# Half of the gate/up pairs of two SwiGLU up projections by seven block products in place of eight

## The reference, cut to what matters

```python
def rms_norm_2(x, g):
    xf = x.astype(jnp.float32)
    y = xf * lax.rsqrt(jnp.mean(xf * xf, axis=-1, keepdims=True) + RMS_EPS)
    return (y * g.astype(jnp.float32)).astype(x.dtype)

def swiglu_ffn(h, w13, w2):
    g, u = jnp.split(h @ w13, 2, axis=-1)
    return (jax.nn.silu(g) * u) @ w2

h = h + swiglu_ffn(rms_norm_2(h, conv_ffn_norm_g[i]), conv_ffn_w13[i], conv_ffn_w2[i])
h = h + swiglu_ffn(rms_norm_2(h, mla_ffn_norm_g[j]), mla_ffn_w13[j], mla_ffn_w2[j])
```

## Time and profile before

| | |
|---|---|
| Time, median of three runs | 1853.58 us (1853.45 to 1859.59) |
| The profiled execution's own time | 1854.15 us |
| Its span, first to last instruction | 1852.3 us |
| TensorE busy | 1821.4 us, 98% |
| VectorE, ScalarE, GpSimd busy | 50%, 39%, 11% |
| Granted TensorE clock, mean | 0.997 of full |
| DMA, mean | 87 GB/s |
| Up stage of feed-forward two | about 923 to 1163 us |
| Up stage of feed-forward three | about 1480 to 1721 us |

### The profile page before, as it was taken

How to read it: one execution, slowest core, us unless ns; L and a number is a source line. 1 busy time by engine, 2 the same in 40 slices (tenths; PEclk the granted TensorE clock), 3 DMA queues, 4 the chain that set the end, 5 groups by cost and what they waited for, 6 DMA issues and landing times.

```text
span 1852.3 us, 27361 instructions
## 1 busy us (share of the span) xinstructions
PE 1821.4 (98%) x10063; PEld 1474.8 (80%) x10063; DVE 918.4 (50%) x1280; ACT 716.5 (39%) x1059; POOL 203.5 (11%) x178
## 2 busy tenths in 40 slices
...
DMA packets 309228, 161.03 MB, mean 87 GB/s; under 512 B 12688, under 2 KB 306832, under 8 KB 309024
## 3 DMA queue, kind: packets, MB, share of 16 engines
...
## 4 chain that ended last, share of the span: by engine, by line
PE 96%; DVE 2%; ACT 1%; issue 1%; DMA 0%; ACTq 0%; DVEq 0%
PE ps L372 28%; PE ps L374 28%; PE ps L373 28%; PE ps L1796 1%; PE ps L1207 1%; PE ps L2109 1%; PE ps L2110 1%; PE ps L1787 1%; PE ps L1118 1%; PE ps L1524 1%; PE ps L940 1%; PE ps L1468 1%; PE ps L1512 0%; PE ps L1893 0%; PE ps L1894 0%
## 5 line engine op out<-in xcount | busy, mean ns | idle before, releaser
L372 PE MATMUL ps<-xhi,whi 128*128 128x512 f32 x1656 | 653.6, 395 | 2.3 <-ACT mx L1442 1.2
L374 PE MATMUL ps<-xhi,wlo 128*128 128x512 f32 x1656 | 645.3, 390 | 0.0
L373 PE MATMUL ps<-xlo,whi 128*128 128x512 f32 x1656 | 645.0, 389 | 0.0
L359 ACT ACTIVATE whi<-raw 128x1024 fp32r<-128x1024 f32 (+2 forms) x297 | 309.0, 1040 | 709.3 <-PE ps L374 708.8
L367 DVE TENSOR_TENSOR wlo<-raw,whi 128x1024 fp32r<-128x1024 f32 (+2 forms) x297 | 365.5, 1231 | 270.0 <-ACT whi L359 270.0
L372 PEld LDWEIGHTS ps<-xhi,whi 128*128 128x128 f32 x1656 | 311.0, 188 | 70.8 <-issue 4.4
L373 PEld LDWEIGHTS ps<-xlo,whi 128*128 128x128 f32 x1656 | 311.1, 188 | 65.9 <-issue 3.4
L374 PEld LDWEIGHTS ps<-xhi,wlo 128*128 128x128 f32 x1656 | 311.0, 188 | 65.2
L638 DVE TENSOR_TENSOR zS<-ps,rs 128x512 f32<-128x512 f32 x132 | 91.3, 692 | 293.1 <-PE ps L374 284.3
L374 PE MATMUL ps<-h_hi,wlo 128*128 128x512 f32 x528 | 205.4, 389 | 0.0
L372 PE MATMUL ps<-h_hi,whi 128*128 128x512 f32 x528 | 205.4, 389 | 0.0
...
## 6 DMA issues: line engine op xcount, KB each, us to landing
raw<-in_conv_ffn_w SPq DMA_DIRECT2D x52, 512.0 KB, 3.8
raw<-in_mla_ffn_w SPq DMA_DIRECT2D x52, 512.0 KB, 3.9
raw<-in_w_up SPq DMA_DIRECT2D x44, 512.0 KB, 3.8
raw<-in_w_in SPq DMA_DIRECT2D x28, 512.0 KB, 3.8
raw<-in_conv_w_in SPq DMA_DIRECT2D x24, 512.0 KB, 3.8
...
```

What stands on the lines that cost most here:

```text
L359: a.activation(whi[:, u % PARTS, 0:n], raw[:, u % RAW, 0:n], ACT.Copy).then_inc(hi_split, 1)
L372: t_.matmul(out, wh, xh, start=first, stop=False)
L373: t_.matmul(out, wh, xl, start=False, stop=False)
L374: return t_.matmul(out, wl, xh, start=False, stop=last)
```

## The change

Both up stages now take their pairs alternately in two ways. Of 22 pairs, the first two and the last two are multiplied as before, and between them a loop of nine passes (`SEVEN_END` = 10) takes one plain pair and one by `pe_seven`. There, the gate and the up unit form a 2x2 block matrix with the halves of the model dimension (`g0`, `g1`, `u0`, `u1`: four slices, 512 elements each), the activations another with the two halves of the tokens (256 each), and Strassen's method in Winograd's form needs seven products m1 to m7 of blocks in place of eight. Each is 4 slices x 3 matmuls on 256 columns.

- Weight sums, per pass: VectorE makes four sums of half units and the remainders, ScalarE two roundings (`dve_w_sums`, `dve_gate_lo`, `dve_last_sum_lo`, `act_seven`).
- x sums t1 to t4, once per stage, from `xT` and the gain, each 4 slices x 256 columns (`act_x_sums`, `dve_x_sums`), then rounding and remainder (`act_x_sums_hi`, `dve_x_sum_lo`). ScalarE does the sums and the rounding of t1, t3, t2 ahead of `act_rstd`, that of t4 inside the stage.
- Block sums, per pass: ScalarE copies m1 out of PSUM, VectorE adds seven times 256 columns, then scales twice by `rs` (`dve_seven`). The seven results lie in the six ring banks of PSUM.
- The products go in fp32 to `h`. The x sums (in the last eight tiles of `h`), `t_hi`, `t_lo`, `w_hi` and `w_lo` lie where `h` and its rounded part come to lie, so rounding (`act_product_hi`, ScalarE) and remainder (`pool_products_late`, POOL, in place over `h`) of all 22 products come behind the loop, during the last four units. The down stages read them there.
- Feed-forward three uses the same buffers as two; its own (`h3_hi`, `h3_lo`) are gone.

The functions below are new; the calls in the engines' lists change accordingly. The calls of feed-forward three change in the same way as those of two, which stand at the end.

```diff
+def w_part(buf, more, u, name):
+    g0, u0 = buf[:, u % PARTS, :], buf[:, (u + 1) % PARTS, :]
+    return {"g0": g0[:, 0:HU], "g1": g0[:, HU:UNIT], "s3": u0[:, 0:HU], "u1": u0[:, HU:UNIT],
+            "s1": more[:, 0, :], "s2": more[:, 1, :], "s4": more[:, 2, :]}[name]
+def x_part(name):
+    if name in X_SUMS:
+        n = X_SUMS.index(name)
+        return [b[:, n, :, :] for b in (t_hi, t_lo)]
+    k0, c0 = {"x11": (0, 0), "x21": (4, 0), "x22": (4, HT)}[name]
+    return [b[:, k0:k0 + 4, c0:c0 + HT] for b in (xhi, xlo)]
+def seven_bank(stage, n):
+    b, at = {"m1": (0, 0), "m6": (1, 0), "m2": (1, HT), "m5": (2, 0), "m3": (3, 0), "m7": (4, 0), "m4": (5, 0)}[n]
+    return ring(S.bank(f"{stage} bank{b}"))[:, at:at + HT]
+def pe_seven(pe, stage, it):
+    u, n0 = FIRST[stage] + 2, TILE0[stage]
+    def multiply(n, w, x):
+        (xh, xl), wh, wl = x_part(x), w_part(whi, w_hi, u, w), w_part(wlo, w_lo, u, w)
+        for k in range(4):
+            cols = slice(k * P, (k + 1) * P)
+            last = passes(seven_bank(stage, n), wh[:, cols], wl[:, cols], xh[:, k, :], xl[:, k, :],
+                          k == 0, k == 3)
+        return last
+    pe.wait_ge(acc_free, n0 + 2 + 4 * it)
+    pe.wait_ge(sums_lo, nth(stage, it, 2) + 2)
+    multiply("m1", "g0", "x11").then_inc(block_done, 1)
+    multiply("m6", "s2", "t2")
+    multiply("m5", "s1", "t1").then_inc(block_done, 1)
+    multiply("m2", "g1", "x21").then_inc(unit_used, 1)
+    pe.wait_ge(lo_split, u + 4 * it + 1)
+    multiply("m3", "s4", "x22").then_inc(block_done, 1)
+    pe.wait_ge(lo_split, u + 4 * it + 2)
+    multiply("m7", "s3", "t3").then_inc(block_done, 1)
+    multiply("m4", "u1", "t4").then_inc(unit_used, 1)
+def pe_up_seven(pe, stage, name, gain, residual):
+    n0 = TILE0[stage]
+    pe_pair(pe, stage, 0, None, False, parts_of(gain), lambda: pe_sum(pe, name, NORM0[residual]))
+    for n in range(NRING):
+        pe_ring(pe, f"{stage} bank{n}")
+        S.at[f"{stage} bank{n} taken"] = ("acc_free", n0 + 2 * FT + 2)
+    pe_pair(pe, stage, 2, None, True)
+    for n in X_SUMS:
+        pe.wait_ge(*after(f"{stage} {n} lo"))
+    with pe.Fori(1, SEVEN_END) as it:
+        pe_pair(pe, stage, 0, it, False)
+        pe_seven(pe, stage, it)
+    for odd in range(2):
+        pe_pair(pe, stage, 4 * SEVEN_END + 2 * odd, None, odd)
+def act_x_sums(act, stage, gain):
+    act.wait_ge(unit_used, FIRST[stage])
+    act.wait_ge(acc_free, TILE0[stage] + 2)
+    for k in range(4):
+        last = a.activation(tf["t3"][:, k, :], xT[:, k, HT:T], ACT.Copy, scale=par(gain, k))
+    last.then_inc(*step("act", f"{stage} x12"))
+    act.wait_ge(*after(f"{stage} d1"))
+    for k in range(4):
+        last = a.activation(tf["t1"][:, k, :], tf["t1"][:, k, :], ACT.Copy, scale=par(gain, k))
+    last.then_inc(*step("act", f"{stage} t1"))
+def act_x_sums_hi(act, stage, names):
+    for n in names:
+        act.wait_ge(*after(f"{stage} {n}"))
+        a.activation(t_hi[:, X_SUMS.index(n), :, :], tf[n], ACT.Copy).then_inc(*step("act", f"{stage} {n} hi"))
+def dve_x_sums(dve, stage, gain):
+    dve.wait_ge(unit_used, FIRST[stage])
+    dve.wait_ge(acc_free, TILE0[stage] + 2)
+    v.tensor_tensor(tf["t1"], xT[:, 0:4, HT:T], xT[:, 0:4, 0:HT],
+                    ALU.subtract).then_inc(*step("dve", f"{stage} d1"))
+    for name, c0, less, ready in (("t3", HT, "t3", "x12"), ("t2", HT, "t1", "t1"), ("t4", 0, "t2", "t2")):
+        dve.wait_ge(*after(f"{stage} {ready}"))
+        for k in range(4):
+            last = v.scalar_tensor_tensor(tf[name][:, k, :], xT[:, 4 + k, c0:c0 + HT], par(gain, 4 + k),
+                                          tf[less][:, k, :], ALU.mult, ALU.subtract)
+        last.then_inc(*step("dve", f"{stage} {name}"))
+def dve_x_sum_lo(dve, stage, n):
+    dve.wait_ge(*after(f"{stage} {n} hi"))
+    at = X_SUMS.index(n)
+    v.tensor_tensor(t_lo[:, at, :, :], tf[n], f32(t_hi[:, at, :, :]),
+                    ALU.subtract).then_inc(*step("dve", f"{stage} {n} lo"))
+def act_seven(act, stage, it, zS, yg):
+    u, n0 = FIRST[stage] + 2, TILE0[stage]
+    split_hi(act, u - 1, it, 4)
+    act.wait_ge(sums_made, nth(stage, it, 4) + 2)
+    a.activation(w_hi[:, 0:2, :], xg[:, :, :], ACT.Copy).then_inc(sums_hi, 1)
+    split_hi(act, u, it, 4)
+    act_silu_gate(act, stage, 0, it, 0, zS, yg)
+    act.wait_ge(sums_made, nth(stage, it, 4) + 4)
+    a.activation(w_hi[:, 2, :], raw[:, u % RAW, HU:UNIT], ACT.Copy).then_inc(sums_hi, 1)
+    split_hi(act, u + 1, it, 4)
+    act.wait_ge(block_done, nth(stage, it, 4) + 1)
+    a.activation(kept["m1"], seven_bank(stage, "m1"), ACT.Copy).then_inc(block_kept, 1)
+    split_hi(act, u + 2, it, 4)
+    act_silu_gate(act, stage, 2, it, 1, zS, yg)
+def act_up_seven(act, stage, h, h_hi, zS, yg):
+    u0 = FIRST[stage]
+    a.preload_act_table_set("silu_and_others")
+    for j in range(4):
+        if j < 3:
+            split_hi(act, u0 + j + 2)
+        if j % 2 == 0:
+            act_silu_gate(act, stage, j, None, j // 2, zS, yg)
+        if j == 0:
+            act_x_sums_hi(act, stage, ("t4",))
+    with act.Fori(1, SEVEN_END) as it:
+        act_seven(act, stage, it, zS, yg)
+    u = 4 * SEVEN_END
+    split_hi(act, u0 + u + 1)
+    for j, tiles in enumerate((range(0, 6), range(6, 12), range(12, 17), range(17, 21))):
+        for m in tiles:
+            act_product_hi(act, stage, m, h, h_hi)
+        split_hi(act, u0 + u + j + 2)
+        if j % 2 == 0:
+            act_silu_gate(act, stage, u + j, None, j // 2, zS, yg)
+    act_product_hi(act, stage, FT - 1, h, h_hi)
+def pool_products_late(pool, stage, h, h_hi, h_lo):
+    for m in range(FT):
+        pool.wait_ge(prod_hi, PAIR0[stage] + m + 1)
+        g.tensor_tensor(h_lo[:, m, :], h[:, m, :], f32(h_hi[:, m, :]), ALU.subtract).then_inc(prod_lo, 1)
+def dve_w_sums(dve, stage, it):
+    u = FIRST[stage] + 2
+    gate, up = raw[:, u % RAW, :], raw[:, (u + 1) % RAW, :]
+    for n in range(2):
+        dve.wait_ge(unit_loaded[(u + n) % RAW], in_loop(LOADED[u + n], it, 64 // RAW))
+    v.tensor_tensor(xg[:, 0, :], up[:, 0:HU], up[:, HU:UNIT], ALU.add).then_inc(sums_made, 1)
+    dve.wait_ge(sums_made, nth(stage, it, 4) + 1)
+    v.tensor_tensor(xg[:, 1, :], xg[:, 0, :], gate[:, 0:HU], ALU.subtract).then_inc(sums_made, 1)
+    v.tensor_tensor(up[:, 0:HU], gate[:, 0:HU], up[:, 0:HU], ALU.subtract).then_inc(sums_made, 1)
+    dve.wait_ge(sums_hi, nth(stage, it, 2) + 1)
+    v.tensor_tensor(w_lo[:, 0:2, :], xg[:, :, :], f32(w_hi[:, 0:2, :]), ALU.subtract).then_inc(sums_lo, 1)
+def dve_gate_lo(dve, stage, it):
+    u = FIRST[stage] + 2
+    part = raw[:, u % RAW, HU:UNIT]
+    dve.wait_ge(hi_split, u + 4 * it + 1)
+    v.tensor_tensor(wlo[:, u % PARTS, :], raw[:, u % RAW, :], f32(whi[:, u % PARTS, :]),
+                    ALU.subtract).then_inc(sums_lo, 1)
+    dve.wait_ge(sums_lo, nth(stage, it, 2) + 2)
+    v.tensor_tensor(part, part, xg[:, 1, :], ALU.subtract).then_inc(sums_made, 1)
+def dve_last_sum_lo(dve, stage, it):
+    u = FIRST[stage] + 2
+    dve.wait_ge(sums_hi, nth(stage, it, 2) + 2)
+    v.tensor_tensor(w_lo[:, 2, :], raw[:, u % RAW, HU:UNIT], f32(w_hi[:, 2, :]),
+                    ALU.subtract).then_inc(lo_split, 1)
+def dve_seven(dve, stage, it, h, zS, yg):
+    u = FIRST[stage] + 2
+    d0, a0 = nth(stage, it, 4), nth(stage, it, 7)
+    split_lo(dve, u - 1, it, 4)
+    dve_w_sums(dve, stage, it)
+    dve_up_unit(dve, stage, 0, it, 0, 0, zS)
+    dve_gate_lo(dve, stage, it)
+    dve_last_sum_lo(dve, stage, it)
+    dve_up_unit(dve, stage, 0, it, 1, 0, zS)
+    dve_product(dve, stage, 0, it, 0, h, zS, yg)
+    split_lo(dve, u + 1, it, 4)
+    dve.wait_ge(block_kept, nth(stage, it, 1) + 1)
+    dve.wait_ge(unit_used, u + 4 * it + 1)
+    v.tensor_tensor(kept["u2"], seven_bank(stage, "m6"), kept["m1"], ALU.add).then_inc(block_added, 1)
+    v.tensor_tensor(zS[:, 0, 0:HT], seven_bank(stage, "m2"), kept["m1"], ALU.add).then_inc(block_added, 1)
+    dve.wait_ge(block_added, a0 + 1)
+    v.tensor_tensor(kept["u4"], seven_bank(stage, "m5"), kept["u2"], ALU.add).then_inc(block_added, 1)
+    split_lo(dve, u + 2, it, 4)
+    dve.wait_ge(block_done, d0 + 3)
+    dve.wait_ge(block_added, a0 + 3)
+    v.tensor_tensor(zS[:, 0, HT:T], seven_bank(stage, "m3"), kept["u4"], ALU.add).then_inc(block_added, 1)
+    dve.wait_ge(block_added, a0 + 4)
+    v.tensor_tensor(zS[:, 0, :], zS[:, 0, :], rs[:, :], ALU.mult).then_inc(acc_free, 1)
+    dve.wait_ge(block_done, d0 + 4)
+    v.tensor_tensor(kept["u3"], seven_bank(stage, "m7"), kept["u2"], ALU.add).then_inc(block_added, 1)
+    dve.wait_ge(block_added, a0 + 5)
+    v.tensor_tensor(zS[:, 1, HT:T], seven_bank(stage, "m5"), kept["u3"], ALU.add).then_inc(block_added, 1)
+    dve.wait_ge(unit_used, u + 4 * it + 2)
+    v.tensor_tensor(zS[:, 1, 0:HT], seven_bank(stage, "m4"), kept["u3"], ALU.add).then_inc(block_added, 1)
+    dve.wait_ge(block_added, a0 + 7)
+    v.tensor_tensor(zS[:, 1, :], zS[:, 1, :], rs[:, :], ALU.mult).then_inc(acc_free, 1)
```

(57 more changed lines are left out.)

49 lines of the change are left out of this document (39 added, 10 removed).

## The result

| | before | changed |
|---|---|---|
| Median (lowest to highest), runs | 1854.09 us (1853.45 to 1859.59), 6 | 1864.81 us (1860.70 to 1870.79), 6 |
| Profiled execution, its span | 1854.15, 1852.3 us | 1870.79, 1868.7 us |
| Busy TensorE, VectorE, ScalarE, GpSimd | | 98, 58, 41, 12% |
| Granted clock, mean | 0.997 | 0.99 |

What follows compares the result with a forecast made beforehand. TensorE's matmul time, or a new wait of TensorE, was taken to bound the kernel. 1854.15 − 14.4 (pairs) + 14.95 (stands) + 3.4 (low clock) = 1858.1 us, range 1843 to 1870.

Steps and rivals of the forecast that it cites:

- slower by over 0.5%: Whole kernel: outcome given chance 0.28, from POOL, weight loads, VectorE, and longer starts or low clock.
- within 0.5%: Whole kernel: outcome given chance 0.57, a time that measurement cannot tell from no change (9.3 us).
- a stand at a down stage's first tile: Down stages: TensorE waiting at the first output tile, named beforehand as a sign that the prediction is wrong.
- Spacing c: Loop: time between starts of 256-column matmuls, taken as 0.120 us, making a pass 20.96 us.
- Gain of 18 pairs: Loops of both up stages: a pair takes 10.08 us instead of 10.88, saving 14.4 us over 18.
- First stands: Ahead of unit 2 in each up stage: TensorE waits 4.75 us in feed-forward two, 6.3 in three.
- Second stands: Before the loop in each up stage: TensorE waits 1.95 us for the last x remainder (t4).
- Low clock: Behind each long stand: 3.4 us at half clock, costing 1.7 us per stage, 3.4 in all.
- POOL at the down stages: End of each up stage: POOL's 22 remainders finish at 34.7 us, needed at 36.0, so hidden, costing nothing.
- the two rivals on c: Loop: extra shrinks with columns, c 0.110 to 0.115, chance 0.28; weight loads set pace, 0.125 to 0.15, chance 0.10.
- The sum of 12.3 us: Start of each up stage: chain from x difference through x sums, norm and unit 2's weight remainder, 12.3 us.
- The rival: Down stages: POOL late at first output tile if subtractions average over 1.55 us; 11.4 us at 1.81; chance 0.15.

Runs made afterwards that it cites:

- E9: Kernel before, matmuls of one stage cut into four of 128 columns, of another into 384 and 128: 1907.67 us in a single execution.
- E1: Changed kernel with the roundings of t1, t3 and t2 moved behind the rounding of unit 2's weights: 1854.41 us, ratio 1.0015 to the kernel before.
- E3: E1 and E2 together on the changed kernel, with ScalarE's table load first and x sums spread later: 1840.78 us, 0.9940 of the kernel before.
- E2: Changed kernel with TensorE's wait for the x remainders moved into the loop, ahead of the seven products: 1857.72 us, ratio 1.0022 to the kernel before.
- E4: E3 with the remainders of product tiles 0 to 2 on VectorE, the other 19 on POOL: 1838.62 us, 0.9925 of the kernel before.

## Why the prediction was right, and where it was not

The time fell into the range. Of the three cases the median is, by 0.05%, in "slower by over 0.5%", which had 0.28, and the interval reaches well into "within 0.5%", which had 0.57. All that was missed is on the same side. By the prediction's own signs, one part of it was wrong: "a stand at a down stage's first tile" was named as such a sign, and it came in both stages. The terms, as forecast and as measured:

| Term | Forecast | Measured |
|---|---|---|
| Spacing c, pass | 0.120, 20.96 us | 0.120, 20.98 us |
| Gain of 18 pairs | 14.4 | 14.0 |
| First stands | 4.75, 6.3 | 4.76, 6.35 |
| Second stands | 2 x 1.95 | 2 x 2.45 |
| Low clock (profiled execution) | 3.4 | 6.2 |
| POOL at the down stages | 0 | 2.8 |
| Change | +3.95 | +11.0 (medians: +10.7) |

The gain is 0.4 smaller since four plain units less a pass are 0.78, not 0.80.

**Right.** "So it is either a fixed delay that the slow stream hides (c = 0.1067 + 0.0133 = 0.120) or a limit on columns per ns": the number is the first one's, and the two rivals on c fall. There was some luck in it: the choice leaned on the fp32 rows, whose extra is 0.003 and not 0.0133, and no run shows that the two have one cause. The rule of the Trainium skill, TensorE: Matmul & The Clock Gate, section on packing small matmuls, that a weight load overlaps a running matmul only where the row groups differ, would, as an estimate, have made 0.214; the row shows 0.120, and E9 0.112 even at 128 columns, so the measurement decides against it here. The first stands came out to within 0.05 us at both stages, from rows of the same instructions, added in ScalarE's order. VectorE kept up in the loop (75% busy where I had 79: summed, its durations are 16.6 us of a pass, where I had 16.5, but those of consecutive instructions overlap a little).

**One link of the chain was another.** The sum of 12.3 us is right partly by luck. In it VectorE's four subtractions for t2 (1.7) and the rounding of t2 (1.06) follow the scaling of t1. The rows:

```profile
935.00 1.67 DVE L763 SCALAR_TENSOR_TENSOR h<-xT,pcol,h 128x256 f32<-128x256 f32 x4 [0.19 <-ACT h L747]
935.00 2.96 ACT L753 ACTIVATE t_hi<-h 128x1024 fp32r<-128x1024 f32 x3
```

t2 was ready at 936.67, while ScalarE rounded t1, t3 and t2 one after another until 937.95. So the path ran through three roundings (2.96), 0.2 longer than the link that I had, and handovers shorter than the 0.05 that I took for each made up for it. E1 takes just these 2.96 away.

**Low clock: mis-sized.** The step "If each long stand is followed by such a stretch, it costs 1.7 us per stage" took one stretch's length, 3.4 us, from the earlier trace rows and let it follow the long stands alone. Behind those it was 6.8 us long, and it follows a stand of 4.8 and 6.35 us (2.8 and 1.8 us) and in the profiled execution one of the two of 2.45 us as well (1.6). The term was 2.8 short; its upper bound, twice 3.4, holds it. E1 to E3 show it as part of the price of the stands: in E3's profile neither stands nor low clock are left at the starts.

**Second stands: 0.5 short each.** I began at the moment the next matmul was wanted and added the drain, the remainder and 0.05. Passage of the last matmul (its drain starts 0.20 us after the next one would have) and 0.42 from the remainder's end to the first matmul were left out:

```profile
958.25 0.69 DVE L854 TENSOR_TENSOR zS<-ps,rs 128x512 f32<-128x512 f32 x1 [1.93 <-PE ps L382]
958.86 1.22 DVE L770 TENSOR_TENSOR t_lo<-h,t_hi 128x1024 fp32r<-128x1024 f32 x1
```

958.05 + 0.20 + 0.61 + 1.22 + 0.42 = 960.50.

**POOL: the margin was too thin to call hidden.** "0.36 more for one overlapped VectorE operation of 0.73, so for the 9 us of VectorE work here 4.4 more, 34.7. Hidden, with 1.3 to spare." It ended 35.36 + 1.9 = 37.3 us after the loop, 1.3 late. The rival named the point, 1.55 us on average: it was 1.607, and 22 x 0.057 = 1.3 per stage is the price seen (1.4). What failed is the size of the contention: an overlapped operation with two inputs in SBUF cost POOL up to 1.0 us, not 0.36, and it slowed VectorE alike, which I had not counted. The rival was right in its mechanism and its point, at a quarter of the price at its bound (5.7 per stage).

**Not seen.** That the stands need not exist. I costed the wait ahead of the loop as a price of the change, where it was one of its place (E2), and likewise ScalarE's order (E1, E3). With both removed, and the tail (E4), the loop's gain is left whole.
